# A decoder layer on one core: the experts' down products and scatters move one body later

## The reference

```python
def hier_moe(xn, router_group, router_expert, w_gate, w_up, w_down):
    ...
    y = jnp.zeros_like(xn)
    for g in range(N_GROUPS):
        hg = jax.nn.silu(jnp.einsum('nd,edf->nef', xn, w_gate[g])) * jnp.einsum('nd,edf->nef', xn, w_up[g])
        y = y + jnp.einsum('nef,efd->nd', hg * combine[:, g, :, None], w_down[g])
    return y
```

## Time and profile before

| | us |
|---|---|
| median of 3 runs | 671.91 (671.87 to 672.01) |
| span of the profiled execution | 669.8 |
| TensorE busy in it | 650.2 (97%) |
| DVE busy | 390.7 (58%) |
| ScalarE busy | 215.9 (32%) |
| transfers | 138.72 MB, 52.8% of 16 engines' span on SP's queue |

### The profile page before, as it was taken

How to read it: one execution, slowest core, us unless ns; L and a number is a source line. 1 busy time by engine, 2 the same in 40 slices (tenths; PEclk the granted TensorE clock), 3 DMA queues, 4 the chain that set the end, 5 groups by cost and what they waited for, 6 DMA issues and landing times.

```text
span 669.8 us, 10196 instructions
## 1 busy us (share of the span) xinstructions
PE 650.2 (97%) x3969; PEld 466.9 (70%) x3969; DVE 390.7 (58%) x736; ACT 215.9 (32%) x448; POOL 101.4 (15%) x138
## 2 busy tenths in 40 slices
PE   5799999999999999999989999999999999999998
PEld 3579999988888888888779995354544445453535
DVE  4648335678897878785674667453443535251615
ACT  6346232234534444422435565302020201110112
POOL 3300015899300000000000010110110101010010
PEclk9899999999999999999999999999999999999999
DMA  7432223202232121112345057999999999999943
GB/s 242 147 125 65 64 65 97 92 1 64 79 100 74 60 68 52 68 44 90 126 166 243 33 219 284 381 408 412 401 422 397 423 394 420 407 418 404 417 185 126
DMA packets 49794, 138.72 MB, mean 207 GB/s; under 512 B 6202, under 2 KB 28235, under 8 KB 41556
## 3 DMA queue, kind: packets, MB, share of 16 engines
q1 hardware_dynamic: 47298, 134.37, 52.8%
q0 software_dynamic: 2304, 3.64, 1.5%
q10 hardware_dynamic: 146, 0.07, 0.0%
HBM read 138.62 MB, written 4.19 MB: 213 GB/s over the span
## 4 chain that ended last, share of the span: by engine, by line
PE 87%; DVE 6%; ACT 3%; issue 2%; DMA 1%; POOL 0%; ACTq 0%; DVEq 0%
PE bank L990 16%; PE bank L608 12%; PE bank L609 12%; PE bank L610 12%; PE bank L1004 8%; PE bank L1114 8%; PE bank L850 1%; DVE y_lo L1903 1%; PE bank L1015 1%; PE bank L877 1%; PE bank L874 1%; ACT whi L1233 1%; DVE sig_a L1617 1%; DVE sig_a L1613 1%; DMA wraw<-in_w_out 1%
## 5 line engine op out<-in xcount | busy, mean ns | idle before, releaser
L990 PE MATMUL bank<-w_pair,xgT 128*64 128x512 f32 x512 | 113.8, 596 | 0.0
L990 PEld LDWEIGHTS bank<-w_pair,xgT 128*64 128x64 f32 x512 | 35.2, 137 | 66.4 <-issue 65.4
L1547 DVE TENSOR_TENSOR wlo<-wraw,whi 128x2048 fp32r<-128x2048 f32 (+1 forms) x25 | 56.4, 2258 | 20.3 <-ACT whi L1233 20.3
L608 PE MATMUL bank<-whi,xhi 128*128 128x256 f32 x224 | 64.4, 288 | 0.0
L609 PE MATMUL bank<-wlo,xhi 128*128 128x256 f32 x224 | 63.0, 281 | 0.0
L610 PE MATMUL bank<-whi,xlo 128*128 128x256 f32 x224 | 62.9, 281 | 0.0
L608 PE MATMUL bank<-xhi,whi 128*128 128x512 f32 x152 | 61.4, 404 | 0.0
L609 PE MATMUL bank<-xlo,whi 128*128 128x512 f32 x152 | 60.1, 396 | 0.0
L610 PE MATMUL bank<-xhi,wlo 128*128 128x512 f32 x152 | 59.7, 393 | 0.0
L1004 PE MATMUL bank<-w_pair,hT 128*64 128x512 f32 x256 | 58.1, 595 | 0.0
L1880 DVE SCALAR_TENSOR_TENSOR hg<-bank,pair_w,hs 128x256 f32<-128x256 f32 x16 | 7.7, 483 | 80.6 <-ACT hs L1452 80.6
(11 more groups left out here) (331 smaller groups left out, 1330.9 us busy)
## 6 DMA issues: line engine op xcount, KB each, us to landing
w_pair<-in_expert_w_gate SPq DMA_DIRECT2D x32, 1024.0 KB
w_pair<-in_expert_w_up SPq DMA_DIRECT2D x32, 1024.0 KB
w_pair<-in_expert_w_down SPq DMA_DIRECT2D x32, 1024.0 KB, 17.4
wraw<-in_w_in SPq DMA_DIRECT2D x17, 1024.0 KB, 5.6
wraw<-in_w_out SPq DMA_DIRECT2D x4, 1024.0 KB, 5.3
h<-in_x SPq DMA_DIRECT2D x4, 512.0 KB, 5.3
wraw<-in_w_gla_branch SPq DMA_DIRECT2D x2, 1024.0 KB, 5.0
wraw<-in_w_attn_branch SPq DMA_DIRECT2D x2, 1024.0 KB, 5.2
```

What stands on the lines that cost most here:

```text
L608: nc.tensor.matmul(ps, lhi(k), rhi(k), start=(k == 0), stop=False)
L990: last = nc.tensor.matmul(tiles[GU_BANK[s]][j * SLOT:(j + 1) * SLOT, :].rearrange("p (f n) -> p f n", f=2), xgT[:, k, s * P + j * SLOT:s * ...
L1547: nc.vector.tensor_tensor(wl, raw, wh.bitcast(F32), ALU.subtract).then_inc(s_lo, 1)
```

## The change

From body 1 on, the down products of a body are issued in the next body, behind its gate/up products, and every scatter one body after its own. Body 0 still has its own down products. So body 1 has no down products, bodies 2 to 6 have those of the body before, and body 7 has those of body 6, ahead of its gate/up products, and later its own. The hidden transposes of both sides stand together, slot products and flips come after the scatter, and the slot products of body 0 come after all 32 products of its first half. The one-hots get a second buffer, and banks are dealt out anew. `y_hi`, `y_lo` and the additions move with the products they belong to. SP's order of requests is the same in bodies 1 to 6; each down request waits for the products that have moved. For body 7 the down weights of body 6 are asked for between the two sides of gate and up.

```diff
-H_BANK = (2, 3)
+H_BANK = 5
 DOWN_BANKS = ((4, 5), (6, 7))
-ROWS_BANKS = (0, 1, 2, 3)
-W_BANKS = (4, 7)
-OH_BANK = (5, 6)
+ROWS_BANKS = (0, 1, 3, 2)
+W_BANK = 2
+OH_BANK = 3
 SCATTER_BANKS = (4, 7, 5, 6)
+LATE_BANKS = (4, 7, 0, 6)
...
-        onehot = more("onehot", [P, NB, 2 * P], BF16)
+        onehot = [more(f"onehot{i}", [P, NB, 2 * P], BF16) for i in range(2)]
...
-        flipped = [tiles[k][:, 0:2 * P].bitcast(BF16) for k in OH_BANK]
+        flipped = [tiles[OH_BANK][:, s * 2 * P:(s + 1) * 2 * P].bitcast(BF16) for s in range(2)]
+        def slots(j, s):
+
+            c = 32 * (j % 2) + 16 * s
+            return tiles[W_BANK][:, c:c + 8]
...
+        def scatter_bank(i, u):
+
+            if i + 1 == BODIES:
+                return tiles[LAST_BANKS[u]]
+            return tiles[LATE_BANKS[u % 4] if i + 2 == BODIES else SCATTER_BANKS[u % 4]]
+
+        def hidden_bank(s):
+            return tiles[H_BANK][:, s * 2 * P:(s + 1) * 2 * P]
...
+                    slot_values(1)
+                    for s in range(2):
                         last = slot_matmul(s, 0, 2, 8)
                     last.then_inc(s_pwm, 1)
...
-                for i in range(BODIES):
-                    n = r * BODIES + i
-
-                    pe.wait_ge(s_xgT[0], n + 1)
-                    pe.wait_ge(s_wgu[0], 64 * n + 64)
-                    expert_gate_up(i, 0, 0)
-                    if i == 0:
-                        first_slot_weights()
...
-                            pe.wait_ge(s_ohT[s], n + 2)
-                    pe.wait_ge(s_hT[0], n + 1)
-                    pe.wait_ge(s_wd[0], 32 * n + 32)
-                    expert_down(0, 0)
-                    pe.wait_ge(s_hg[1], n + 1)
-                    hidden_transposes(1)
-                    expert_down(0, 1).then_inc(s_down[0], 1)
-                    pe.wait_ge(s_hT[1], n + 1)
-                    pe.wait_ge(s_wd[1], 32 * n + 32)
-                    expert_down(1, 0)
-                    expert_down(1, 1).then_inc(s_down[1], 1)
...
+                def hidden(n):
+
+                    for s in range(2):
+                        pe.wait_ge(s_hg[s], n + 1)
+                        hidden_transposes(s)
+
+                def down(i, n):
+
+                    for s in range(2):
+                        pe.wait_ge(s_hT[s], n + 1)
+                    for s in range(2):
+                        pe.wait_ge(s_add[s], 2 * n + 1)
+                        pe.wait_ge(s_add[s + 2], 2 * n + 1)
+                        pe.wait_ge(s_wd[s], 32 * n + 32)
+                        expert_down(s, 0)
+                        expert_down(s, 1).then_inc(s_down[s], 1)
...
+                def scatter(i, n):
+
                     for s in range(2):
                         pe.wait_ge(s_ylo[s], n + 1)
                     for u in range(8):
                         b, half = u // 2, u % 2
+                        if u == 2 and i + 2 == BODIES:
+                            hidden(n + 1)
+                        elif u == 2:
+                            for s in range(2):
+                                pe.wait_ge(s_hT[s], n + 2)
                         if u >= 4:
                             pe.wait_ge(s_add[u % 4], 2 * n + 2)
                         cols_ = slice(half * 512, (half + 1) * 512)
                         for s in range(2):
                             for part in (y_hi, y_lo):
-                                last = nc.tensor.matmul(tiles[SCATTER_BANKS[u % 4]][:, :], onehotT[i % 3][s][:, b, :],
+                                last = nc.tensor.matmul(scatter_bank(i, u)[:, :], onehotT[i % 3][s][:, b, :],
...
+
+                for i in range(BODIES):
+                    n = r * BODIES + i
+
+                    if i + 1 == BODIES:
+                        down(i - 1, n - 1)
+                    pe.wait_ge(s_xgT[0], n + 1)
+                    pe.wait_ge(s_wgu[0], 64 * n + 64)
+                    expert_gate_up(i, 0, 0)
+                    pe.wait_ge(s_xgT[1], n + 1)
+                    expert_gate_up(i, 0, 1).then_inc(s_gu[0], 1)
+                    if i == 0:
+                        first_slot_weights()
+                        for s in range(2):
+                            pe.wait_ge(s_ohT[s], n + 1)
+                        onehot_transposes(1)
+                    pe.wait_ge(s_xgT[2], n + 1)
+                    pe.wait_ge(s_xgT[3], n + 1)
+                    pe.wait_ge(s_wgu[1], 64 * n + 64)
+                    expert_gate_up(i, 1, 0)
+                    expert_gate_up(i, 1, 1).then_inc(s_gu[1], 1)
+                    if 2 <= i < BODIES - 1:
+                        down(i - 1, n - 1)
+                    if i >= 1:
+                        pe.wait_ge(s_ylo[0], n)
+                    if i + 1 < BODIES:
+                        hidden(n)
+                    if i == 0:
+                        pe.wait_ge(s_pw, n + 2)
+                        slot_values(2)
+                        for s in range(2):
+                            pe.wait_ge(s_ohT[s], n + 2)
+                        onehot_transposes(2)
+                        down(0, n)
+                    if i + 1 < BODIES:
+                        ahead = 2 if i == 0 else 1
+                        pe.wait_ge(s_pw, n + ahead + 1)
+                        for s in range(2):
+                            pe.wait_ge(s_ohT[s], n + ahead + 1)
+                        row_transposes(i + 1)
+                    if i >= 1:
+                        scatter(i - 1, n - 1)
+                    if i >= 1 and i + 2 < BODIES:
+                        pe.wait_ge(s_xgT[3], n + 2)
+                        slot_values(i + 2)
+                        pe.wait_ge(s_xgT[2], n + 2)
+                        onehot_transposes(i + 2)
+                    elif i + 1 == BODIES:
+                        for s in range(2):
+                            pe.wait_ge(s_oh[s], n + 2)
+                            slot_matmul(s, 0, 0, 2).then_inc(s_tkm[s], 1)
+                        onehot_transposes(0)
+                        down(i, n)
+                        for s in range(2):
+                            pe.wait_ge(s_idx[s], n + 2)
+                            pe.wait_ge(s_ohT[s], n + 2)
+                        last_scatter(i, n)
+                        row_transposes(i + 1)
...
-
-                for s in range(2):
+            def next_gate_up(i, n, sides=(0, 1)):
+
+                for s in sides:
                     sp.wait_ge(s_gu[s], n)
                     load(2 * i + s, s, True)
+
+            def next_down(i, n):
+
                 for s in range(2):
                     sp.wait_ge(s_down[s], n)
                     load(2 * i + s, s, False)
+
+            def bodies_after_first(n):
+
+                next_gate_up(1, n + 1)
+                next_down(1, n + 1)
+                next_gate_up(2, n + 2)
+                with sp.Fori(2, BODIES - 2) as i:
+                    next_gate_up(i + 1, n + i + 1)
+                    next_down(i, n + i)
+                last = BODIES - 1
+                next_gate_up(last, n + last, (0,))
+                next_down(last - 1, n + last - 1)
+                next_gate_up(last, n + last, (1,))
+                next_down(last, n + last)
...
-            with sp.Fori(1, BODIES) as i:
-                reload(i, i)
+            bodies_after_first(0)
...
+                for i in range(BODIES):
+                    n = r * BODIES + i
+                    if i + 1 == BODIES:
+                        high_rows(n - 1)
+                    for s in range(2):
+                        act.wait_ge(s_gu[s], n + 1)
+                        nc.scalar.activation(hs[s][:, :], tiles[GU_BANK[s]][:, 0:FF], ACT.Silu).then_inc(s_silu[s], 1)
+                        if s == 0 and i == 0:
+                            onehot_out(1, n + 1)
+                    if 2 <= i < BODIES - 1:
+                        high_rows(n - 1)
+                    for s in range(2):
+                        hidden_out(s, n)
+                    if i + 2 < BODIES:
+                        onehot_out(i + 2, r * BODIES + i + 2)
+                    elif i + 1 == BODIES:
+                        onehot_out(0, n + 1)
+                    if i == 0 or i + 1 == BODIES:
+                        high_rows(n)
...
+                next_onehots(1)
                 slot_weights(0)
-                next_onehots(1)
+                slot_weights(1)
+                next_onehots(2)
                 for i in range(BODIES):
                     n = r * BODIES + i
+                    if i + 1 == BODIES:
+                        low_rows(n - 1)
                     dve.wait_ge(s_pw, n + 1)
                     for s in range(2):
...
-                        if s == 0 and i == 0:
-                            slot_weights(1)
-                            next_onehots(2)
-                        if s == 0 and i + 2 < BODIES:
-                            slot_weights(i + 2)
-                        elif s == 0 and i + 1 == BODIES:
```

(38 more changed lines are left out.)

130 lines of the change are left out of this document (39 added, 91 removed).

## The result

The changed kernel takes 674.74 us (median of 8 runs, 673.23 to 675.72), the kernel before, measured again beside it, 672.25. The ratio is 1.0037, 95% interval 1.0027 to 1.0047: 2.5 us slower, where no difference and at most 674.0 had been forecast. The runs of the changed kernel lie in two groups, spans of 671.4 to 672.3 and of 673.4 to 673.9, the latter with a lower mean clock; the profiled run, with a span of 671.4, is the shortest of them. The kernel before has a span of 669.8.

The account below looks back on a forecast made before the run. TensorE was taken to bound the kernel, barely ahead of the transfers. Its 6.2 us gain less 5.9 of new wait in body 2 gave -0.3, hence 671.6, plus 0.3 for thin margins: 671.9 us, range 669.8 to 674.0.

Parts of the forecast that it names:

- What bounds the kernel: Expert stretch: TensorE needs 32.05 us per body, transfers 31.7, so TensorE leads by only 0.3.
- TensorE's own gain: Expert bodies: removed waits 1.24 and 2.9, breaks 4.9, less 2.8 of new waits; about 6.2 us gained by TensorE alone.
- The breaks: Changes of form between gate/up or down and other products: 0.15 out, 0.28 in; 0.7 us saved in each of bodies 1-7.
- The wait in body 2: Body 2's gate/up halves wait for weights, 2.1 and 3.8 us: 5.9 of new wait.
- the bulk of the stream: Gate/up 1, down 1, gate/up 2 and three gather pairs: 22.3 MB from 418.4 at 414 GB/s, until 472.3.
- its end: Body 2's second-half weights: ready at 474.3, bounds 473.0 to 475.3, after start, last-engine and signal allowances.
- the trailing of the last engine: End of body 2's weight stream: last of 16 engines ends about 1.2 us after the mean.
- at nothing: Gather i+2, asked for at the end of body i: lands in 8.7 us, has 20, so no cost.
- the sum's 0.5 for the signal: Body 2's second-half weights: some 0.5 us allowed for the signal, within the 474.3.
- The clock: Rival 1: clock falls to half rate behind body 2's second wait, +1.7 us, 673.5; chance 0.2.
- Body 7 and the margins: Body 7's second-half weights land near 633.5, wanted 635.4; 0.3 us for thin margins; starving rival 674.4, chance 0.05.
- The sum: Whole kernel: -6.2 + 5.9 gives -0.3, span 669.5; final row transposes begin at 665.1; forecast median 671.9 us.

Follow-up runs that it names:

- body 2 was mended: Changed kernel with body 1's down products split in body 2, side 0 ahead of gate/up's first half, side 1 between halves: 0.9992, 671.38 us.

## Why the prediction was wrong, point by point

*What bounds the kernel.* Right. TensorE led before by so little that a gain would meet the transfers; the same bytes left out, worth nothing before and 1.1% after, show it.

*TensorE's own gain*, forecast at 6.2. Without the wait in body 2 (half of down 1 left out) the way from the first gate/up product to the row transposes at the end is 660.80 - 409.49 = 251.3, against 256.0 in the kernel before: 4.7. The missing 1.5 are: bodies 0 and 1, 52.45 instead of 52.1 (0.4); four bodies of 31.03 instead of 30.95 (0.3); body 7, 44.3 instead of 43.4 (0.9): down 6 and gate/up take 21.1 for 20.7, scatter 6 with the hidden transposes 8.0 for 7.7, the last scatter 7.5 for 7.2.

*The breaks.* A body's gain came out at 1.02 for 1.1. The price of one break was mis-sized, 0.25 for 0.43; the sum over a body was still about right, since it had been read from whole blocks.

*The wait in body 2.* The mechanism was right, and the bulk of the stream too: it falls off at 472, as worked out (472.3). The step that failed is its end, 474.3 with bounds to 475.3, where 475.58 was measured. Of these 1.3, some 0.3 are a later start of the experts (409.76 for 409.42). The rest is the end of the stream. The forecast had the bytes of body 3's gathers in its sum, as the third of three pairs, 1.1 us; but it took the trailing of the last engine from the stream's end at 645, where no gather runs, and it priced the gather, now asked for at the end of a body, "at nothing", with only its own deadline in view. It did not ask what the gather does to the weights beside it: after body 1 the requests, at 463.3 and 465.3, bring it into the last transfers for body 2, and there it costs 1.5 to 2.0. With the gathers asked for later the second half starts at 473.45, where the sum without their 1.1 gives 473.2, and the time is that of the kernel before. A little luck is in that agreement: the sum's 0.5 for the signal stands on no row, and the chains show 0.14 between landing and start (475.58 and 475.72), so the weights trailed some 0.4 to 0.6 longer than the sum had it even without the gathers.

*The clock.* The rival had the price right, 1.7 (8.78 for 7.09), and its chance too low. It was to decide from a wait of 3.9, and the forecast's second wait was 3.8. The fall came behind 2.21 in one run, and behind 4.06 and 4.84 in two other kernels; it stayed away behind 2.53 in the first of these, and behind 2.98 with the late gathers. That the later weights made the second wait long enough in part of the changed kernel's runs is likely from these figures but not shown. The Trainium skill's page "TensorE: Matmul & The Clock Gate", section "Why this matters for your kernels", advises against longer idle gaps between matmul bursts because of this fall. The falls behind 4.06 and 4.84 agree, and filling both gaps with 25 extra products won 1.3.

*Body 7 and the margins.* Body 7 did not starve, but the last weights of down 6 landed at 626.46 and its second side began at 627.0. As soon as body 2 was mended, TensorE waited 3.2 there.

*The sum.* The row transposes at the end begin at 667.47 where 665.1 had been worked out: 1.4 from the start of body 2's second half (475.72 for 474.3), 0.3 from bodies 2 to 6, and 0.6 from body 7. That alone would have stayed in the range: the profiled run took 673.23, 1.3 above the forecast. The median lies another 1.5 above this run. Filling both waits wins 1.3, so most of that can be put down to the clock in body 2; a part has nothing to do with the change, since the kernel before's median, too, lies 0.9 above its shortest run. The range failed at its upper end because the late landing and the clock stood in the forecast as alternatives, each with a time of its own, and here they came together.

## What to carry to other kernels

When an engine leads the transfers by one per cent, a reordering on that engine is worth what the transfers let through: lay the requests and landings beside the order, body by body, before counting saved gaps. A transfer that is moved has two prices, its own deadline and what it does to the transfers beside it, which can be more than its bytes; look for the moment at which a stream's last bytes are waited for and keep gathers away from it. An unavoidable wait is the place to put moved work, and the next wait that this uncovers has to be mended in the same step.

## What the runs showed of the hardware

Two gathers, 0.51 MB together, delayed the last weights of a full stream by 1.5 to 2.0 us (three runs with the gathers early, one with them late), where their bytes take 1.2 at 414 GB/s. TensorE's clock fell to 0.50 behind an idle time of 2.21 us, and did not fall behind one of 2.53 us nine microseconds later, nor behind 2.98 in another run; behind 4.06 and 4.84 it fell. So in these runs the length of a wait alone does not tell, and a fall is to be counted as a chance.
